# Expert loop of a mixture-of-experts encoder block: visits of 192 rows, tails behind pairs of chunks, drains counted apart

## The reference

```python
logits = ht @ router_w + router_b                 # 32 experts
top_vals, top_idx = lax.top_k(logits, 4)
gates = softmax(top_vals)
gu = xb @ w_up[e] + b_up[e]                       # 1024 x 2048
x_glu = minimum(gu[:, :1024], 7); x_lin = clip(gu[:, 1024:], -7, 7)
hid = x_glu * sigmoid(1.702 * x_glu) * (x_lin + 1)
ys = hid @ w_down[e] + b_down[e]                  # 1024 x 1024
out[token] += gate * ys
```

## Time and profile before

| | us |
|---|---|
| median of 3 runs | 2546.52 |
| lowest, highest | 2540.04, 2547.19 |
| span of the profiled execution | 2545.7 |
| TensorE busy in it | 2319.0 (91%) |
| VectorE busy | 1875.6 (74%) |
| ScalarE busy | 1324.2 (52%) |
| GpSimd busy | 369.2 (15%) |

### The profile page before, as it was taken

The page is one execution under the profiler, slowest core; times in us unless marked ns, Lnnn a source line. Parts: engine busy times, 40 slices in busy tenths (PEclk is TensorE's granted clock), DMA queues, the critical chain, the costliest instruction groups (busy, mean ns, idle before and its releaser), DMA issues.

```text
span 2545.7 us, 43546 instructions
## 1 busy us (share of the span) xinstructions
PE 2319.0 (91%) x15432; PEld 1801.3 (71%) x15433; DVE 1875.6 (74%) x2044; ACT 1324.2 (52%) x1489; POOL 369.2 (15%) x321
## 2 busy tenths in 40 slices
PE   6999996599978977999999999999999999999992
PEld 4889874498846966777777767677666677777761
DVE  4599878614043266888988888888888888998883
ACT  5412264403142135666766665666666667766663
POOL 0000000010002102121212212122122122222121
PEclk8999997699999968999999999999999999999996
DMA  4211311311101036999989888899888999999895
GB/s 143 66 50 51 100 52 35 115 60 34 50 17 30 26 135 236 331 310 346 358 291 305 290 299 292 257 347 303 296 279 288 305 333 353 356 326 337 287 313 180
DMA packets 275264, 546.24 MB, mean 215 GB/s; under 512 B 11420, under 2 KB 45520, under 8 KB 274832
## 3 DMA queue, kind: packets, MB, share of 16 engines
q1 hardware_dynamic: 259648, 495.66, 55.1%
q0 software_dynamic: 13632, 46.54, 7.8%
q10 hardware_dynamic: 1904, 2.90, 0.4%
HBM read 506.39 MB, written 38.67 MB: 214 GB/s over the span
## 4 chain that ended last, share of the span: by engine, by line
PE 74%; DVE 10%; issue 8%; ACT 4%; DMA 3%; ACTq 0%; DVEq 0%; POOLq 0%; SPq 0%; POOL 0%
PE PS L2529 12%; PE PS L2530 11%; PE PS L2092 9%; PE PS L2532 9%; PE PS L2543 7%; PE PS L2324 4%; PE PS L2422 4%; DVE wlo L1889 3%; PE PS L2524 3%; PE PS L2131 2%; DMA raw<-in_exp_w_up 2%; ACT whi L1129 1%; PE PS L2496 1%; PE PS L2561 1%; PE PS L2384 1%
## 5 line engine op out<-in xcount | busy, mean ns | idle before, releaser
L1889 DVE TENSOR_TENSOR wlo<-raw,whi 128x2048 fp32r<-128x2048 f32 x411 | 932.0, 2286 | 122.5 <-ACT whi L1129 100.4
L1129 ACT CAST whi<-raw 128x2048 fp32r<-128x2048 f32 x411 | 777.9, 1911 | 146.2 <-PE PS L2543 48.7
L2529 PE MATMUL PS<-whi,xhi 128*128 128x512 f32 x1088 | 460.7, 423 | 1.3 <-DVE wlo L1889 1.2
L2530 PE MATMUL PS<-wlo,xhi 128*128 128x512 f32 x1088 | 424.9, 391 | 0.0
L2532 PE MATMUL PS<-whi,xlo 128*128 128x512 f32 x816 | 321.3, 394 | 0.0
L2529 PEld LDWEIGHTS PS<-whi,xhi 128*128 128x128 f32 x1088 | 206.3, 190 | 67.4 <-issue 23.9
L2529 PE MATMUL PS<-whi,hhi 128*128 128x512 f32 x544 | 223.5, 411 | 12.4 <-DVE wlo L1889 12.4
L2530 PEld LDWEIGHTS PS<-wlo,xhi 128*128 128x128 f32 x1088 | 205.6, 189 | 40.2
L2530 PE MATMUL PS<-wlo,hhi 128*128 128x512 f32 x544 | 215.0, 395 | 0.0
L2532 PEld LDWEIGHTS PS<-whi,xlo 128*128 128x128 f32 x816 | 153.6, 188 | 35.5
L2532 PE MATMUL PS<-whi,hlo 128*128 128x512 f32 x408 | 160.7, 394 | 0.0
(11 more groups left out here) (398 smaller groups left out, 4342.1 us busy)
## 6 DMA issues: line engine op xcount, KB each, us to landing
raw<-in_exp_w_up SPq DMA_DIRECT2D x275, 1024.0 KB, 7.2
raw<-in_exp_w_down SPq DMA_DIRECT2D x136, 1024.0 KB, 7.1
ring<-in_w_in SPq DMA_DIRECT2D x11, 1024.0 KB, 5.4
xres<-in_x SPq DMA_DIRECT2D x4, 1024.0 KB, 10.2
ring<-in_xattn_wk SPq DMA_DIRECT2D x4, 1024.0 KB, 9.1
ring<-in_xattn_wv SPq DMA_DIRECT2D x4, 1024.0 KB, 6.3
ring<-in_w_out SPq DMA_DIRECT2D x4, 1024.0 KB, 7.0
xres<-in_x SPq DMA_DIRECT2D x1, 4096.0 KB, 19.1
```

The costliest lines, as they stand in the source:

```text
L1129: nc.scalar.copy(whi[:, chunk_slot(c, NSPL), :], raw[chunk_slot(c, NRAW)][:]).then_inc(s_whi, 1)
L1889: nc.vector.tensor_tensor(wlo[:, chunk_slot(c, NSPL), :], raw[chunk_slot(c, NRAW)][:], whi[:, chunk_slot(c, NSPL), :].bitcast(F), ALU.subtract
L2529: pe.matmul(o, hi[:, k, :], wh, start=begins and kk == 0 and bias is None, stop=False)
L2530: pe.matmul(o, hi[:, k, :], wl, start=False, stop=False)
```

## The change

A visit takes up to 192 rows, with a tail of none, 32 or 64 rows (flag 0, 1, 2). A tail of 64 goes in two column groups, whole contraction each, so that nothing has to be added; VectorE reads it straight from PSUM. The tail's products stand behind a pair of chunks instead of behind each. The drains of main rows and of tail rows are counted by two semaphores; the first bias product waits for the main count, the tail block for the tail count. SyncE takes a raw buffer of a visit without a tail as free when VectorE has split it, and one of a visit with a tail when its pair has been multiplied. In the last turn the chunks loaded ahead are those of the last down product. Gather and scatter move 128 + 64 rows in every visit.

```diff
-CAP = P + TAIL
+CAP = P + 2 * TAIL
...
+        def wait_tails(eng, t, c):
+            wait_multiplied(eng, t, c | 1)
...
+            def next_loads(t, eu, en, now, last):
+                def loads(load, e):
+                    with sp.If(now >= 1):
+                        for c in range(2):
+                            load(t + 1, c, c, e, wait_tails)
+                    with sp.Else():
+                        for c in range(2):
+                            load(t + 1, c, c, e, wait_lo)
...
+                with sp.If(t < last_):
+                    loads(load_up, en)
+                with sp.Else():
+                    loads(load_down, eu)
...
-                    for c in range(3, 12):
-                        load_chunk(t, c, eu, ed)
-                    for c in range(3):
-                        load_chunk(t + 1, c, en, ed)
+                    flag = has_tail(t + 1)
+                    with sp.If(before >= 1):
+                        first_loads(t, eu, wait_tails)
+                    with sp.Else():
+                        first_loads(t, eu, wait_lo)
+                    with sp.If(now >= 1):
+                        more_loads(t, eu, ed, wait_tails)
+                    with sp.Else():
+                        more_loads(t, eu, ed, wait_lo)
+                    next_loads(t, eu, en, now, last)
...
-                        for c in range(15, 19):
-                            load_chunk(last_, c, None, e_last, last=True)
+                        load_down(t, 3, 3, expert(t - 1), wait_tails)
...
-                for b, rows in ((0, P), (1, TAIL)):
+                for b, rows in ((0, P), (1, 2 * TAIL)):
...
-            step(nc.vector.tensor_scalar(exi[:, 0, :], exi[:, 1, :], 13.0, None, ALU.mult))
-            step(nc.vector.tensor_scalar(exi[:, 1, :], exi[:, 0, :], 6, None, ALU.arith_shift_right))
+            step(nc.vector.tensor_scalar(exi[:, 0, :], exi[:, 1, :], 43.0, None, ALU.mult))
+            step(nc.vector.tensor_scalar(exi[:, 1, :], exi[:, 0, :], 7, None, ALU.arith_shift_right))
...
+            step(nc.vector.scalar_tensor_tensor(out=vb, in0=vb, scalar=-float(TAIL), in1=v_edge,
+                                                op0=ALU.add, op1=ALU.is_gt))
+            step(nc.vector.tensor_tensor(v2, v2, vb, ALU.add))
...
+            for h in range(2):
+                step(nc.vector.tensor_copy(wide_gate[2 * TAIL * h:2 * TAIL * (h + 1), :],
+                                           pairs(PS[0:2 * TAIL, 4, NB:2 * NB])))
...
+                if tail == 2:
+                    for h in range(2):
+                        ins = nc.vector.tensor_scalar(glu[0:2 * TAIL, 1, HALF * h:HALF * (h + 1)],
+                                                      PS[2 * TAIL * h:2 * TAIL * (h + 1), 1, 0:HALF], LIMIT, None,
+                                                      ALU.min)
...
+            def pair(t, c, i, flag, hi, lo, tl, bias=None, tails_drained=None):
+                o = PS[:, 2 * (i % 2), :]
...
+                for half in range(2):
+                    wait_lo(pe, t, c + half)
...
+                    if half == 0:
+                        last_main(3, slot).then_inc(s_wmm, 1)
                 with pe.If(flag >= 1):
+                    last_main(KT - 1, slot)
+                    if tails_drained is not None:
+                        pe.wait_ge(s_ytl, tails_drained)
...
+                    with pe.If(flag >= 2):
+                        part = [PS[2 * TAIL * h:2 * TAIL * (h + 1), 2 * (i % 2) + 1, 0:HALF] for h in range(2)]
...
+                        for k in range(KT):
+                            chunk = raw[chunk_slot(c + k // 4, NRAW)]
+                            for h in range(2):
+                                ins = pe.matmul(part[h], tl[:, k, :], chunk[:, k % 4, cols[h]],
+                                                start=k == 0 and bias is None, stop=k == KT - 1)
...
-                    if i == 0:
-                        if c0 == 0:
-                            pe.wait_ge(s_yev, 4 * t)
+                    if i < 2 and c0 == 0:
+                        drained = 2 * t - 1 + i
+                        pe.wait_ge(s_yev, drained)
```

More of the change, by code:

```diff
@@ L1138, in turned_hi @@
                 if tail:
[L1139 removed]
+                    rows = TAIL * tail
+                    ins = nc.scalar.copy(tl[:, :, 0:rows], PS[:, 6, 0:KT * rows].rearrange("p (k c) -> p k c", c=rows))
                 ins.then_inc(done, 1)
@@ L1159, in tail_low @@
             def tail_low(t, c, i, tail):
-                if not tail:
+                if tail != 1:
                     if i == 3:
@@ new lines, in tail_rows @@
+                    with dve.Else():
+                        for i in range(2):
+                            dve.wait_ge(s_low, 6 * t + low + i)
+                            for h in range(2):
+                                rows, c0 = slice(TAIL * h, TAIL * (h + 1)), 512 * i + HALF * h
+                                ins = nc.vector.scalar_tensor_tensor(out=yb[0:TAIL, 1, c0:c0 + HALF],
+                                                                     in0=PS[rows, 2 * i + 1, 0:HALF],
+                                                                     scalar=row_gate[rows, bass.ds(2 * t - 1, 1)],
+                                                                     in1=low_dn[rows, i, :], op0=ALU.mult,
+                                                                     op1=ALU.add)
+                            ins.then_inc(s_ytl, 1)
@@ new lines, in pair @@
+                for half in range(2):
+                    wait_lo(pe, t, c + half)
+                    slot = chunk_slot(c + half, NSPL)
+                    for kk in range(4):
+                        k = 4 * half + kk
+                        wh, wl = whi[:, slot, kk, :], wlo[:, slot, kk, :]
+                        pe.matmul(o, hi[:, k, :], wh, start=k == 0 and bias is None, stop=False)
+                        pe.matmul(o, hi[:, k, :], wl, start=False, stop=False)
+                        if kk < 3:
+                            pe.matmul(o, lo[:, k, :], wh, start=False, stop=False)
+                    if half == 0:
+                        last_main(3, slot).then_inc(s_wmm, 1)
@@ new lines, in pair @@
+                    with pe.Else():
+                        part = [PS[TAIL * j:TAIL * (j + 1), 2 * (i % 2) + 1, 0:HALF] for j in range(4)]
+                        if bias is not None:
+                            for h in range(2):
+                                pe.matmul(part[h], SEL[:, 0:TAIL], bias[:, cols[h]], start=True, stop=False)
+                        for k in range(KT):
+                            chunk = raw[chunk_slot(c + k // 4, NRAW)]
+                            for h in range(2):
+                                ins = pe.matmul(part[2 * (k % 2) + h], tl[:, k, 0:TAIL], chunk[:, k % 4, cols[h]],
+                                                start=k == 1 or k == 0 and bias is None, stop=k >= KT - 2)
+                        ins.then_inc(s_wmm, 1)
@@ L2561, in up @@
                     pe.matmul(PS[:, 2 * (i % 2), :], SEL[:], bias, start=True, stop=False)
-                    for half in range(2):
-                        c = c0 + 2 * i + half
-                        wait_lo(pe, t, c)
-                        products(i, both, xhi, xlo, xtl, 4 * half, chunk_slot(c, NSPL), chunk_slot(c, NRAW),
-                                 half == 0, half == 1, bias)
+                    pair(t, c0 + 2 * i, i, both, xhi, xlo, xtl, bias, drained)
             def down(t, both, c0=8, read=2):
@@ L2571, in down @@
                     pe.wait_ge(s_g if i == 0 else s_upr, 2 * t + read)
-                    for half in range(2):
-                        c = c0 + 2 * i + half
-                        wait_lo(pe, t, c)
-                        products(i, both, hhi, hlo, htl, 4 * half, chunk_slot(c, NSPL), chunk_slot(c, NRAW),
-                                 half == 0, half == 1)
+                    pair(t, c0 + 2 * i, i, both, hhi, hlo, htl)
             last_ = pe.value_load(usedb[0:1, 0:1], min_val=0, max_val=NVIS - 1)
```

234 lines of the change are left out of this document (135 added, 99 removed).

## The result

| | before | changed |
|---|---|---|
| median of the runs (4 each), us | 2545.25 | **2843.58** |
| lowest to highest, us | 2540.04 to 2547.19 | 2838.86 to 2852.63 |
| span of the profiled execution, us | 2545.7 | 2837.0 |

What follows compares the result with a forecast made beforehand. TensorE was taken as the bound (97.5% busy in the loop), with DMA close in rows without tails. Terms summed to -109.6 us on the profiled 2545.7, 2436.1, given as 2437 us, range 2408 to 2478.

Steps and rivals of the forecast that it cites:

- Tails behind pairs: TensorE's narrow tail blocks: one per chunk pair costs 2.13 us, saving 31.2 us over 13 visits; added compare taken as nothing.
- Rival C: Even chunk's wait in visits with a tail: pairwise release starves TensorE, slower, about 2600 us; chance 2%.
- Fewer visits: Expert loop: 192 rows a visit leave 32 visits, two second visits removed, -73.6 us.
- D: Routing tables: still count 34 visits, so the 73.6 us stay, 2511 us; chance 3%.
- The 64-row tail: TensorE's wide tail blocks in two visits: two column groups side by side, 3.43 + 0.41 us a pair, +15.6 us.
- B: TensorE's 64-row tail blocks: run one after another, +42 us, 2479 us; chance 8%.
- Drains apart: Before a visit's first bias product: waiting for ScalarE's main drain alone gives -11 us; empty-marker wait taken as nothing.
- Bytes: GpSimd's queue: gather and scatter of 192 rows add 0.8 us in seven rows without tails, +5 us (bounds 0 and 12).
- A: Rows without tails: DMA and VectorE bind next, half the pair gain and all the drain gain lost, 2470 us; chance 20%.
- The queue's waits: SyncE's loads: earlier release without a tail, even chunks one later with a tail, margin 3.6 us; taken as nothing.
- The end: Last down product and after: dead chunks gone, -14.4 us; fewer empty ScalarE turns, -1.7; last visit's tail drain, +0.8.
- E: Rows without tails: earlier queue release lifts them to 36.5 us and waits return whole, 2415 us; chance 9%.

Runs made afterwards that it cites:

- experiment 1: Changed kernel with TensorE's loop ended at the last used visit and the last down product written behind it: 2446.59 us, 0.9616 of before.
- experiments 4 and 6: Changed kernel, loop whole: 4 adds a back-edge prefetch hint to TensorE's loop, 2453 us; 6 puts 222 never executed instructions ahead of it, 2459.66 us.
- by kind (10): Changed kernel with TensorE's loop cut short, second gather and scatter moving 64, 32 or 8 rows by the visit's tail: 2428.1 us, 0.954 of before.
- experiment 11: Changed kernel with TensorE's loop cut short, first two bias products waiting for VectorE's tail rows again: 2461.14 us, 0.9671 of before.
- experiment 9: Changed kernel with TensorE's loop cut short, gather and scatter moving 160 rows a visit instead of 192: 2434.38 us, 0.9576 of before.
- experiment 5: Changed kernel with all five engines' loops ended at the last visit, the last chunk's part behind each: 2446.19 us, 0.9615 of before.
- the padded kernel before: Kernel before the change with 285 never executed products in TensorE's loop, 1711 instructions instead of 1139: 3081.91 us, 1.2123 of before.
- experiment 2: Changed kernel with TensorE's loop cut short, then padded with 172 never executed products to 1680 instructions: 2459.51 us.

## Why the prediction was wrong, and where it was right

**The step that failed** is the sentence in "Tails behind pairs": "The second branch inside the tail adds a compare per pair ... I take nothing". It priced the branch by its own 0.17 us and not by the code behind it. No step counted TensorE's program, though the copies of each pair's block for 64 rows and of the transposes were plain in the diff. The forecast weighed a rule on the time of a compare and branch; the rule that mattered is about where instructions come from. The loop went from six blocks to eight, and that cost 2843.6 - 2446.6 = 397 us. Between the profiled spans it is 390.3 (2837.0 less 2446.7), 386.5 of it between the first index copy and the last, in the windows view of the changed kernel

```profile
1004.73:2753.74 1749.01, 1377.77 (x8142) 1066.26 (x8143) 1197.48 (x1033) 890.80 (x758) 266.29 (x248) 0.88 0.76 252
```

and of experiment 1:

```profile
1006.64:2369.15 1362.51, 1320.48 (x8018) 1017.78 (x8143) 1190.44 (x1033) 882.97 (x758) 278.66 (x247) 0.99 0.94 320
```

TensorE is busy 57.3 us longer for the same products, at the lower clock, and idle 329.2 us longer (371.2 against 42.0). That is 362.6 for instructions less 33 of other waits that vanish: in the pauses the queues and the splits catch up. No rival had it. Rival C, the slower side, was another mechanism: neither the even chunk's wait nor the splits end TensorE's pauses.

**With the loop kept, 2446.6 was measured (experiment 1) where 2437 was forecast**, 9.6 off; with the code of the change whole and the loop kept (experiments 4 and 6) it is 2453 and 2460. Point by point, on the profiled spans (2545.7 to 2446.7, -99.0 against -109.6): the loop gives -89.4, ahead of it -3.9, which lies within what that stretch varies by from run to run, and behind it -5.8. Mean rows by kind:

| rows | before | forecast | cut short (1) | by kind (10) |
|---|---|---|---|---|
| without tails | 37.5 | 38.3 | 39.3 | 37.6 |
| down tail | 42.7 | 41.4 to 41.9 | 42.7 | 42.0 |
| up tail, narrow | 47.0 | 44.9 to 45.4 | 45.2 | 44.8 |
| both, narrow | 52.7 | 49.1 | 48.7 | 48.6 |

By the forecast's values, with the rows of the wide tails at 52.6 (52.9 by the same terms, less a quarter microsecond for the drain), the loop would be about 1317 us. It is 1328.1, 11 more, about what the bytes took beyond their +5.

- **Fewer visits**: right, 32 visits, 384 splits. D falls.
- **Tails behind pairs**: right. In experiment 1's timeline the last main product before a block starts at 2374.06, the second after it at 2376.58:

```profile
2374.06 0.39 PE L2630 MATMUL PS<-whi,hlo 128*128 128x512 f32 x1
2374.38 1.93 PE L2668 MATMUL PS<-raw,htl 128*32 128x256 f32 x32
2376.24 0.50 PE L2638 MATMUL PS<-whi,hhi 128*128 128x512 f32 x1
2376.58 0.40 PE L2639 MATMUL PS<-wlo,hhi 128*128 128x512 f32 x1
...
2396.70 0.39 PE L2630 MATMUL PS<-whi,hlo 128*128 128x512 f32 x1
2397.02 3.67 PE L2657 MATMUL PS<-raw,htl 128*64 128x256 f32 x32
2400.62 0.50 PE L2638 MATMUL PS<-whi,hhi 128*128 128x512 f32 x1
2400.96 0.40 PE L2639 MATMUL PS<-wlo,hhi 128*128 128x512 f32 x1
```

  2.52 less two pitches of 0.227 is 2.07 a pair; 2.13 was forecast. The compare's own 0.17 us is not seen in it.
- **The 64-row tail**: right. 4.26 - 0.45 = 3.81 a pair against 3.84. The groups run side by side, and B falls.
- **Drains apart**: 7 to 14 us against 11, but the wrong waits: it was to come from VectorE's tail rows, 6 of it in the rows with both tails, and none from the marker. In experiment 11 the rows with both narrow tails lose nothing and the whole loss stands in rows that wait for the marker. So far as the size fits, it is luck. Experiment 11 undoes the term in the new order of tails, though: the 15.8 us that the kernel before waits for tail rows are gone there all the same, and which part of the change took them away was not tried.
- **Bytes**: mis-sized. +5 was taken (bounds 0 and 12); the loop gives 15.5 when the rows go back to 160 (1328.08 to 1312.54). The rows without tails (eight stay, not seven) were put 0.8 up and came 1.9 up, with those of experiment 9 still 0.6 over before; the rows with a down tail, taken as covered by TensorE, stand at a DMA share of 0.97 to 0.99 and weren't. This is the first part of A, the DMA share in the rows without tails; the halves that A took from the pairs and the drains were not lost.
- **The queue's waits**: nothing was taken, and the rows with both tails show no loss. The earlier release without a tail, also taken at nothing, carries 40 us against pairs everywhere; how it compares with the kernel before's wait for each chunk was not tried alone.
- **The end**: the dead chunks are gone; behind the loop -5.8 against the -7.6 that its terms and the wide tail of the last visit (+7.7) make. The empty turns (-1.7) were worth nothing: experiment 5.
- **E and the range**: the rows without tails rose instead of falling to 36.5, so E is out. The range of 2408 to 2478 was said to take in B, whose own time is 2479; it took in none of the loss that came.

## What to carry to other kernels

Count the code of a register loop on each engine, in every branch, taken or not, before adding a version of a block to it, and look at where it lies: moving this loop by 222 instructions that never run made 384 us of difference. Watch the instruction queue's packets; a loop that holds shows none in its middle. If it doesn't hold, move what runs once behind the loop, or give the back edge a hint, before judging the change itself; and where queues are full, price rows that "cost nothing because TensorE covers them" by their DMA share.

## What was not expected of the hardware

- By the fitted count, TensorE's loop is kept over seven blocks of 256 instructions and lost over eight, wholly: about eight packets a turn, 12 to 16 us (362.6 in 30 waits; 522.1 in 33 in the padded kernel before).
- The hint on the back edge removes it at the same size and place (2453.5 us, 62 packets). Kept loops near the limit still pause once, after their first turn (4.4 us in experiment 2, 6.3 in 4).
- The branch itself shows it: 6.2 us at the median where it takes 0.2.
- After the pause the clock is granted at 0.51 for 13 products.
- Two column groups of 64 run side by side at half the rate of four of 32, and going in and out of either costs about the same: 3.81 less 3.43 and 2.07 less 1.72 leave 0.38 and 0.35 us a pair (an estimate, from 32 records at 0.107 and at 0.0535 us).
